# Three transformer passages on one core: attention products and compressing nets in plain fp32, and the norm passages rearranged

## The reference, cut to what matters

```python
for layer in range(2):
    h = h + (moba_nsa_mixer if layer == 0 else fox_mixer)(rmsnorm(h, mix_norm[layer]), ...)
    h = h + relu(rmsnorm(h, mlp_norm[layer]) @ w1)**2 @ w2          # inner width 4096
h = rmsnorm(h, final_norm)
mod = silu(c) @ w_ada + b_ada                                       # nine vectors of 1024
h = h + 0.5*gt1 * swiglu(modulate(rmsnorm_2(h, g_ffn1), sh1, sc1))  # inner width 2816
h = h + gt2 * hybrid_mixer(modulate(rmsnorm_2(h, g_mix), sh2, sc2)) # pooling and 8 heads
h = h + 0.5*gt3 * swiglu(modulate(rmsnorm_2(h, g_ffn2), sh3, sc3))
out = rmsnorm_2(h, g_final)
```

## Time and profile before

| | |
|---|---|
| median of three runs | 1181.17 us (1180.4 to 1182.65) |
| profiled execution, its own time | 1180.62 us |
| its span in the profile | 1178.8 us |
| PE, DVE, ACT, POOL busy | 1115.2, 797.0, 588.0, 98.9 us |
| mean granted clock of TensorE | 0.989 |
| read from HBM | 234.58 MB, 200 GB/s over the span |

### The profile page before, as it was taken

One profiled execution on the slowest core, in us unless ns is written; L12 is line 12 of the kernel. 1 busy time (PEld: TensorE's weight loads), 2 busy tenths in 40 slices (PEclk: granted clock), 3 DMA queues, 4 the chain that ended last, 5 costly groups with the idle time before them and its releaser, 6 DMA issues.

```text
span 1178.8 us, 17948 instructions
## 1 busy us (share of the span) xinstructions
PE 1115.2 (95%) x7334; PEld 1013.0 (86%) x7334; DVE 797.0 (68%) x1220; ACT 588.0 (50%) x886; POOL 98.9 (8%) x208
## 2 busy tenths in 40 slices
PE   6899898999999999989999889999998998999997
PEld 5888787999987998789999769999987986999996
DVE  5796656888887676588887775445566666554555
ACT  5775656343436777553433454333345756333342
POOL 3021111111100012000110010000000010000000
PEclk9999999999999999999999989999999999999999
DMA  7642225888884633568888735555553323555551
GB/s 282 240 156 100 72 103 220 306 300 320 297 297 175 245 114 108 172 260 317 302 313 302 305 118 179 179 183 191 196 181 131 136 96 140 185 193 195 178 180 71
DMA packets 39074, 236.84 MB, mean 201 GB/s; under 512 B 4389, under 2 KB 4549, under 8 KB 15952
## 3 DMA queue, kind: packets, MB, share of 16 engines
q1 hardware_dynamic: 26640, 188.76, 44.2%
q0 software_dynamic: 12064, 46.26, 11.4%
q10 hardware_dynamic: 288, 0.67, 0.2%
HBM read 234.58 MB, written 1.10 MB: 200 GB/s over the span
## 4 chain that ended last, share of the span: by engine, by line
PE 78%; DVE 10%; ACT 6%; DMA 3%; issue 2%; SPq 0%; POOL 0%; DVEq 0%; ACTq 0%
PE bank L1337 25%; PE bank L1338 24%; PE bank L1339 24%; DVE w_lo L922 3%; DMA raw<-in_stream 3%; ACT w_hi L604 1%; PE bank L1506 1%; DMA silu_row<-in_c_row 1%; PE bank L1494 1%; PE bank L1495 1%; DVE shifted L1006 1%; ACT shifted L668 1%; DVE w_lo L933 1%; ACT k_two L697 1%; DVE a_lo L1015 1%
## 5 line engine op out<-in xcount | busy, mean ns | idle before, releaser
L1337 PE MATMUL bank<-a_lo,w_hi 128*128 128x256 f32 x1408 | 401.5, 285 | 5.1 <-ACT pair L823 3.0
L1339 PE MATMUL bank<-a_hi,w_hi 128*128 128x256 f32 x1408 | 398.8, 283 | 0.0
L1338 PE MATMUL bank<-a_hi,w_lo 128*128 128x256 f32 x1408 | 398.8, 283 | 0.0
L933 DVE TENSOR_TENSOR w_lo<-raw,w_hi 128x2048 fp32r<-128x2048 f32 x123 | 280.6, 2290 | 167.8 <-ACT w_hi L615 167.6
L615 ACT ACTIVATE w_hi<-raw 128x2048 fp32r<-128x2048 f32 x123 | 235.3, 1916 | 229.9 <-DMA raw<-in_stream 229.8
L1337 PEld LDWEIGHTS bank<-a_lo,w_hi 128*128 128x128 f32 x1408 | 270.5, 192 | 8.8 <-ACT pair L823 3.2
L1338 PEld LDWEIGHTS bank<-a_hi,w_lo 128*128 128x128 f32 x1408 | 270.5, 192 | 1.9
L1339 PEld LDWEIGHTS bank<-a_hi,w_hi 128*128 128x128 f32 x1408 | 270.3, 192 | 0.0
L1337 PE MATMUL bank<-w_lo,hid_hi 128*128 128x512 f32 x432 | 169.0, 391 | 2.0 <-DVE w_lo L933 2.0
L1338 PE MATMUL bank<-w_hi,hid_lo 128*128 128x512 f32 x432 | 168.7, 390 | 0.0
L1339 PE MATMUL bank<-w_hi,hid_hi 128*128 128x512 f32 x432 | 168.1, 389 | 0.0
(11 more groups left out here) (208 smaller groups left out, 1290.4 us busy)
## 6 DMA issues: line engine op xcount, KB each, us to landing
raw<-in_stream SPq DMA_DIRECT2D x177, 1024.0 KB, 5.0
ada_raw<-in_ada POOLq DMA_DIRECT2D x72, 512.0 KB, 8.1
rel_band<-rel_scratch POOLq DMA_DIRECT2D x1, 2048.0 KB, 15.1
cum_row<-cum_scratch POOLq DMA_DIRECT2D x1, 2048.0 KB, 10.6
h<-in_x SPq DMA_DIRECT2D x2, 512.0 KB, 6.5
raw<-in_stream SPq DMA_DIRECT2D x2, 512.0 KB, 7.6
silu_row<-in_c_row POOLq DMA_DIRECT2D x2, 512.0 KB, 5.0
dil_b<-in_dil_bias POOLq DMA_DIRECT2D x1, 1024.0 KB, 13.7
```

What stands on the lines that cost most here:

```text
L933: nc.vector.tensor_tensor(w_lo[:, u % RING, :], raw[:, u % RING, :], w_hi[:, u % RING, :].bitcast(F32), ALU.subtract).then_inc(lo_ready, 2)
L1337: nc.tensor.matmul(dst, l_hi, r_lo, start=start, stop=False)
L1338: nc.tensor.matmul(dst, l_lo, r_hi, start=False, stop=False)
L1339: return nc.tensor.matmul(dst, l_hi, r_hi, start=False, stop=stop)
```

## The change

1. **Products.** Values and turned probabilities stay plain fp32. Heads go in pairs: four fp32 matmuls, the two heads on the two halves of the array's columns. ACT copies the turned probabilities of even heads, DVE those of odd ones; nothing is subtracted. Of the values, ACT copies two pieces and DVE two; the zeros are gone. The heads of the even mixer are listed anew so that each pair shares a kind.
2. **Compressing nets.** Eight plain fp32 matmuls per unit, alternating between the column halves; ACT and DVE add the two sums. These units (`cmp0` to `cmp3`) are not rounded, stand singly between other units, and their sequels move to later ticks. The silu is taken after the turn.
3. **Passages.** POOL rounds the second half of the second unit of every stage behind a passage, and for glu0, uv_dil and glu1 both its halves (`round_second`). ACT scales the first half of the rows; DVE adds the last quarter of `h` ahead of half of the first remainders; there are four buffers of `shifted`. The passage into glu0 weighs the squares by the squared gain instead of squaring twice. `silu_of_c` moves behind the begin of the MLP; of the 72 columns of `mod` 30, 18 and 24 are made in mlp0, mlp1 and glu0.

```diff
@@ PHASES @@
-    ("v_even", 4), ("kcvc", 1), ("kskw", 1), ("nq", 2), ("cmp", 4), ("qm0", 1), ("km0", 1), ("km1", 1), ("qm1", 1),
+    ("v_even", 4), ("kcvc", 1), ("kskw", 1), ("nq0", 1), ("cmp0", 1), ("nq1", 1), ("cmp1", 1), ("qm0", 1), ("cmp2", 1), ("km0", 1),
+    ("cmp3", 1), ("km1", 1), ("qm1", 1),
...
+POOL_HALVES = sorted([2 * FIRST[_name] + 3 for _name in ("mlp0", "v_fox", "mlp1", "glu0", "uv_dil", "glu1")]
+                     + [2 * FIRST[_name] + 2 for _name in ("glu0", "uv_dil", "glu1")])
+NOT_ROUNDED = set(POOL_HALVES) | {2 * FIRST[f"cmp{_j}"] + _part for _j in range(4) for _part in range(2)}
@@ class Tick @@
+        done = part + 1 if parts <= 2 or (tag.startswith("out") and j == 2) else part // 2 + 1
+        self.halves = 2 * (self.u + 2) + (2 if parts == 1 else done)
@@ pool @@
+            def round_second(name):
+                u = FIRST[name] + 1
+                for part in range(2):
+                    if 2 * u + part in POOL_HALVES:
...
+                        pool.tensor_copy(w_hi[:, u % RING, part_], raw[:, u % RING, part_]).then_inc(pool_hi, 1)
+                        pool.wait_ge(pool_hi, n + 1)
+                        pool.tensor_tensor(w_lo[:, u % RING, part_], raw[:, u % RING, part_], w_hi[:, u % RING, part_].bitcast(F32),
+                                           ALU.subtract).then_inc(lo_pool, 1)
@@ act @@
             def round_half():
+                while halves[0] in NOT_ROUNDED:
+                    halves[0] += 1
                 if halves[0] < 2 * N_UNITS:
@@ act, mixer @@
-                    if tick.parts == 2 or tick.part % 2 == 0 or (tick.j == 2 and tick.tag.startswith("out")):
+                    if halves[0] < tick.halves:
                         round_half()
                     for j in tick.t:
-                        nc.scalar.activation(probT_hi[:, j % 2, :], ps[BANK_PT][:, 0:SW], ACT.Copy).then_inc(probsT_hi, 1)
+                        if j % 2 == 0:
...
+                            nc.scalar.activation(probT[:, j % 4, :], ps[BANK_PT][:, 0:SW], ACT.Copy).then_inc(probsT_act, 1)
@@ pe, turn_probs @@
-                    pe.wait_ge(probsT_ready, j)
+                    pe.wait_ge(probsT_dve if j % 2 == 0 else probsT_act, (j + 1) // 2)
@@ pe, products @@
-                three(bank[:, c0:c0 + T], standing(kind, 0, 0, v0), standing(kind, 1, 0, v0), probT_hi[:, j, 0:T],
-                      probT_lo[:, j, 0:T], opens, False)
...
+                for block, lo, hi in ((0, 0, T), (1, T, SW)):
+                    for half in range(2):
+                        j = i - 1 + half
+                        ins = nc.tensor.matmul(ps[ob][HD * half:HD * half + HD, c0 + block * P:c0 + T], v_cols(kind, block, heads[j][3], HD),
+                                               probT[:, j % 4, lo:hi], start=opens and block == 0, stop=i >= NSA and block == 1)
@@ pe, cmp units @@
-                    for k in range(4 * part, 4 * part + 4):
-                        ins = three(ps[4 + v][0:30, 0:256], blk_hi[:, v, 8 * half + k, :], blk_lo[:, v, 8 * half + k, :],
-                                    wh[:, k, :], wl[:, k, :], half == 0 and k == 0, half == 1 and k == 7)
+                    wait_raw(pe, u, 1)
+                    for k in range(8):
+                        row_ = HD * (k % 2)
+                        ins = nc.tensor.matmul(ps[(2, 7)[v]][row_:row_ + 30, 0:256], blk[:, v, 8 * half + k, :], wr[:, k, :],
+                                               start=(half == 0 and k < 2), stop=(half == 1 and k >= 6))
@@ dve, norm_turn @@
-                    turned(name, 0, gain, shift)
-                    rest_half()
-                    add(name, sums, gate, 1, 1)
-                    rest_half()
+                turned(name, 0, gain, shift, (0, 1))
+                add(name, sums, gate, 1, 1)
+                turned(name, 0, gain, shift, (2, 3))
```

More of the change, by code:

```diff
@@ L260, in build @@
         hidc = place("hidc", [P, 2, 2, 32])
+        hidc_e = place("hidc_e", [P, 2, 2, 32])
         pc = place("pc", [P, 16, 16])
@@ L476, in build @@
         GLU_BANKS = ((4, 7), (2, 5))
-        ADA_HALF = N_ADA // 2
+        ADA_OF = {"mlp0": (0, 30), "mlp1": (30, 48), "glu0": (48, N_ADA)}
         def ada_pieces(name, j):
-            first = 0 if name == "mlp0" else ADA_HALF
-            return range(first + ADA_HALF * (j - 2) // (FF1 - 2), first + ADA_HALF * (j - 1) // (FF1 - 2))
+            if name not in ADA_OF:
+                return range(0)
+            (first, last), j0, n = ADA_OF[name], *((1, FF2 - 1) if name == "glu0" else (2, FF1 - 2))
+            return range(first + (last - first) * (j - j0) // n, first + (last - first) * (j - j0 + 1) // n)
         block = ctx.enter_context(nc.Block())
@@ L533, in scale, with modulation_weights @@
                     ins.then_inc(probs_scaled, 1)
-            def modulation_weights(first):
-                pool.dma_start(silu_row[:, :], c_row.partition_broadcast(P)).then_inc(c_landed, 16)
-                for p in range(first, first + ADA_HALF):
+            def modulation_weights(first, last):
+                for p in range(first, last):
                     if p >= ADA_BUFS:
@@ L997, in turned @@
-            def turned(name, t, gain, shift=None):
+                chain(nc.vector.tensor_scalar(b, b, -0.5, 1.5, ALU.mult, ALU.add))
+                nc.vector.tensor_tensor(f[:, 12:14], y, b, ALU.mult).then_inc(inv_ready, 1)
+            def turned(name, t, gain, shift=None, chunks=(0, 1, 2, 3)):
                 m = TURN[name] + 4 * t
                 ts = slice(t * P, (t + 1) * P)
-                for c in range(4):
-                    if shift is not None and c % 2:
+                if shift is not None and chunks[0] == 0:
+                    for c in (1, 3):
@@ L1173, in glu @@
                         hidden_part(x, j % 3)
+                        for p in ada_pieces(name, j):
+                            modulation_column(p)
+                        if (name, j) == ("glu0", FF2 - 1):
+                            gains(("gf2",))
+                        if name == "glu0" and j in (2, 4):
+                            last_norm(j // 2 - 1)
             nc.vector.memset(kc[:, :, :, 15:16].bitcast(F32), 0.0)
@@ L1198, in even_extras @@
                 if tick.at("kcvc", 0, 1):
-                    values("even", (2, 3))
-                if tick.at("nq", 1, 0):
+                    values("even", (2,))
+                if tick.at("nq1", 0, 0):
                     dve.wait_ge(rel_landed, 16)
@@ L1320, in last_root @@
                 inverse_root("last", t)
-                chain(nc.vector.tensor_tensor(fin[:, t, 0:1], stat[:, 5, t:t + 1], stat[:, 6, t:t + 1], ALU.mult))
+                dve.wait_ge(inv_ready, NORM["last"] + t + 1)
             add("last", "glu1", gate_row, 0, 0)
@@ L1587, in even_extras @@
             def even_extras(tick):
-                for v, where in enumerate((("cmp", 3, 0), ("qm0", 0, 1))):
+                for v, where in enumerate((("qm0", 0, 2), ("km1", 0, 1))):
                     if tick.at(*where):
```

483 lines of the change are left out of this document (245 added, 238 removed), and 4 rows, old and new, of the table EVEN_TICKS.

## The result

The changed kernel takes 1164.94 us, median of four runs (1163.88 to 1166.54), against 1181.02 for the kernel before: ratio 0.986, 95% interval 0.985 to 0.988. It is faster, but by 16 us (1.4%) where 38 were forecast, and above the range, which ended at 1158. The profiled execution took 1166.54 us with a span of 1164.7, 14.1 us under that of before.

What follows compares the result with a forecast made beforehand. PE, busy 1115.2 of 1178.8 us, was taken to bound the kernel. Products -15.1, nets -3.8, even mixer's waits +4.7 and passages -23.9 sum to -38.1: 1180.6 becomes 1142.5 us; range from 1125 or a little below to 1158.

Steps and rivals of the forecast that it cites:

- Products: Values times probabilities: four fp32 matmuls per head pair on column halves take 0.80 us; 24 groups save 15.1 us.
- The compressing units: Compressing nets, cmp0 to cmp3: eight fp32 matmuls take 1.87 us a unit instead of 2.84; four units save 3.8 us.
- rival 3: Products and compressing nets: the column halves don't overlap over 128 rows, giving 1167 us; chance 5%.
- The even mixer's new waits: Even mixer: rounding waits for units not yet landed; 9.5 us of waits come, others go, net +4.7 us.
- the fourth rival: Even mixer: new waits let PE's clock fall to 1.2 GHz; slower, 1185 us with 85 us spent there; chance 4%.
- The moved columns: 24 of 72 modulation columns moved into glu0: DVE work where PE has whole units of cover, so no cost.
- POOL: Passages into glu0, uv_dil and glu1: one or two DVE operations slowed by POOL in each, costing 2.8 us.
- rival 2: Passages: POOL is late or stretches DVE, so they give 12 us and the time is 1154; chance 15%.
- The plain passages: Passages into mlp0, mix1 and mlp1: earlier additions and moved roundings and silu waits give 10.1 of 10.45 us back.
- Passage into glu0: Less ACT and DVE work and less lost clock bring 9.2 us; with POOL's contention dealt out, -8.3 us.
- The fox mixer: The mixer between mlp0 and mlp1: forecast change of -5.0 us for the stage.

Runs made afterwards that it cites:

- e1: Changed kernel with nothing rounded in the even mixer's ticks of kskw, cmp0, cmp1 and cmp2, the same halves one to three ticks later: 1143.12 us.
- e9: The kernel before, unchanged, run again for a second profile: 1176.58 us.
- e10: The changed kernel, unchanged, run again for a second profile: 1168.58 us.
- e4: Changed kernel with POOL rounding for the plain passages only; ACT and DVE round the second unit of glu0, uv_dil and glu1 as before: 1165.6 us.
- e3: Changed kernel with glu0's modulation columns and the gains of gf2 made two hidden blocks earlier: 1163.85 us.
- e5: Changed kernel with e1 and e3 together, and the second unit of uv_dil alone rounded by ACT and DVE again: 1137.72 us.
- e6: e5 with no rounding in the one tick ahead of the fox mixer's first head: 1135.19 us.
- e8: e1 with four waits of PE for POOL's memsets put into glu1, ahead of its units 6, 12, 18 and 24: 1166.89 us, one run.

## Why the prediction was wrong

- **Products**: a pair's four matmuls take 0.80 us, as forecast (23 of 24 groups; one ran at the lower clock). What was missed stands ahead of them. The turn of the probabilities takes 0.44 us to the start of the next matmul when fp32 products follow, 0.27 before. The turn and the product behind it, before and then after:

```profile
119.40 0.51 PE L1506 MATMUL bank<-par,prob 128*128 128x128 f32 x3
119.67 0.36 PE L1337 MATMUL bank<-probT_lo,V_all 128*128 128x256 f32 x1
```

```profile
117.77 0.52 PE L1561 MATMUL bank<-par,prob 128*128 128x128 f32 x3
118.21 0.87 PE L1579 MATMUL bank<-probT,V_all 128*64 128x256 f32 x8
```

  24 groups save about 11.2 us instead of 15.1. In all, products and nets of the even mixer shorten its window by about 9 us (it is 7.6 longer, with 7.7 more idle and about 9 more lost to the clock; e1's window gives 8.1), where 11.4 were forecast. Twelve turns at 0.17 us are 2.0 of what is missing. The compressing units take 1.85 us, forecast 1.87; the halves overlap over 128 rows, and rival 3 falls, though its 1167 us are the number nearest to the measured one.
- **The even mixer's new waits** is the step that failed: not by its mechanism, but because its term, +4.7 us, holds idle time alone. The waits themselves were 3.3 (pairs), 3.4 (cmp0, forecast 3.5), 5.6 (cmp1, 4.0) and 1.7 us (cmp2, 2.0). The sum left out that the clock falls with them. I had that as the fourth rival, but only as an all-or-nothing case from 81 us at the lower level; 24 us more of it, some of them while PE waited, cost 9 to 10 us. Of the 14.3 us that the stage is off, this is about 9.3; idle time is 3.0 over the forecast (2.6 of them are the longer wait at kcvc, which e9 and e10 put down in the main to the execution), and products and nets are 2.0 short. e1 shows that waits and clock go together: 24.1 us come back.
- **The moved columns** were priced at nothing because PE has cover inside glu0. At the last block it has none: 3.5 us of columns and 3.4 of gains stand ahead of the additions. 2.8 of the 3.4 are POOL's doing, for in e4 the same gains take 0.6. Columns, gains and POOL's passes together turned -2.9 into +4.4 us; moving the columns gives 3.1 back (e3), silencing POOL 2.4 (e4), and both 7.1 (e5).
- **POOL**: priced at one or two stretched operations in each passage, 2.8 us. The traces show more: DVE's two-input steps of 1, 8 and 512 columns last until POOL's pass ends or half a microsecond longer, and POOL's cast stands still until DVE's remainder ends. That is the second half of rival 2; all the passages together gave 17.1 us instead of 23.9. The row that the prediction built on could have told: its 0.948 us is a mean of 0.55 and 1.35, and the longer one of each two lasted until 0.3 us after POOL's pass.

```profile
677.49 1.81 DVE L994 TENSOR_SCALAR tokn<-tok,fin 128x512 f32<-128x512 f32 x2
677.57 1.45 POOL L577 TENSOR_SCALAR h<-tok,fin 128x1024 f32<-128x1024 f32 x1 [23.66 <-DVE fin L988]
```

  That row reads one tensor, so it isn't a case of two inputs, as the prediction took it. POOL's rounding costs what POOL's help saves in those three passages (e4). POOL was never late: PE did not wait for its w_lo. The Trainium skill says in "GPSIMD Engine Reference", section "Key points", that the two engines contend when VectorE reads two SBUF inputs; the trace agrees (2.24 us for 0.17), and shows that the price is what is left of POOL's pass, not a share of DVE's.
- **The plain passages** went as forecast (-11.4, -10.1): the wait for the vector c is gone, PE is 100% busy in two of three windows. **Passage into glu0**: 7.4 of 8.3.
- **The fox mixer** was not looked at beyond its products. cum_row's 2 MB are issued at 398.2 us against 392.3, where all else is 1.9 us later, and then run beside a unit whose rounding stands ahead of the first logits: a wait of 2.1 us, which e6 takes away. Eight turns at 0.17 us are 1.4 more. That the transfer's lateness came from the store of cum (4.35 us instead of 1.46 to land, beside a unit's transfer) is read from the trace and not tried.

The forecast of 1142.5 us is about what the change gives once its roundings stand where the units have landed: e1 took 1143.1, though by other terms (the even mixer 10.6 us better than forecast in its profile, uv_dil 7 and fox 3 worse), so that the agreement is luck. Two slips in the sums change nothing: 4 x 0.97 us are 3.9 and not 3.8, and the bounds named for the forecast's own range give 1134 to 1152.

## What to carry to other kernels

When instructions are skipped from a fixed order, look at what the freed slot does instead: here it rounded a unit three ahead that was still on its way, with the critical copies behind it. Price a long wait of PE with the clock that goes with it: in this mixer the four waits of 3.1 to 5.6 us each came with 6.8 us at the lower level. Look at the single rows behind a mean before you take it as the price of a contention. And a move into "a stage with cover" is to be followed to its last block, where the cover ends.

## What the runs showed of the hardware

- With PE's waits of 4.2 and 6.2 us in an otherwise full stage the clock was at 1.2 GHz for 3.4 and 6.8 us; behind 1.1 and 3.2 us it was not (e8, one execution). In the even mixer waits of 3.1 to 5.6 us had 6.8 us each after the change, and one of 3.0 us in e10, while the pair wait of 3.0 us before had none. Length alone does not decide it, and what does is open.
- DVE instructions of 1 or 8 columns with two inputs took 1.86 and 2.24 us beside a POOL pass over 1024 columns, 0.22 and 0.17 without; a POOL cast took 3.17 us beside DVE's remainder and 1.03 to 1.50 otherwise. A DVE step of 512 columns with one input in a bank took 0.68 us beside POOL's cast and without it.
- The landing of the same transfer varied by 4 us between executions of the changed kernel and its variants (32.7 to 36.8 us), with a 2 MB transfer beside it.
